# An SSD scan regrouped: 16 steps of two heads and both chunks, with the running sums broadcast by rounded 256-column products

## The chip, the cores and the metric

The kernel runs on one core of a Trainium2 chip. The metric is the device time of one execution in microseconds (us); the time before is the median of 3 runs. Engine names are those of the profile: PE (matrix products; PEld is its weight load), DVE (vector), ACT (scalar, activation functions), POOL (GpSimd), SP (queue of transfers).

## The reference, cut to what matters

The whole program is a transformer block with three mixers (DSA, NSA and SSD) and two further blocks, for 256 tokens of width 1024. The change is in the SSD mixer: 32 heads of 64 channels, 4 groups, state 128, and two chunks of 128 tokens.

```python
a_cum = jnp.cumsum(dtc * a, axis=2)                      # per head, within a chunk
seg = a_cum[:, :, :, None] - a_cum[:, :, None, :]
lmat = jnp.exp(jnp.where(tril, seg, -jnp.inf))           # 128 x 128 per head and chunk
cb = jnp.einsum('bcign,bcjgn->bcijg', cm, bm)            # per group
y_diag = jnp.einsum('bcijg,bcijgh,bcjgh,bcjghp->bcighp', cb, lmat, dtc, xs)
...
y_off = jnp.einsum('bcign,bcghpn,bcigh->bcighp', cm, h_in, jnp.exp(a_cum))
y = y_diag + y_off + xs * d_skip.reshape(SSD_GROUPS, SSD_HPG)[:, :, None]
y = rms_norm(y * jax.nn.silu(z.astype(jnp.float32)), norm_g)
```

`h_in` is zero for the first chunk, so `y_off` exists for the second chunk alone.

## The kernel before, in words

Activations stand transposed, channels on the partitions and the 256 tokens along the free axis, in `arena`. A dense layer is a row of jobs; a job makes 128 output channels out of 8 (`br_ssd`: 16) weight blocks. Each block takes three products of rounded operands (L1835 to L1837: rounded weight by rounded input, rounded weight by the input's remainder, the weight's remainder by rounded input), so a usual job is 24 products of 256 columns. Weights come in units of 8 blocks into a ring of five (`ring`). Two jobs ahead of its use ACT rounds a unit (`ring_hi`, L914), and POOL or DVE makes the remainder (`ring_lo`, L579): POOL for all units of `br_dsa`, POOL and DVE in turns for `mg` and `br_nsa`.

The order of all work is one list, `schedule()`; each engine walks through it and takes its own part of each entry, in order, with waits on semaphores. The stretch of interest has the jobs `mg` 20 to 23 (gates), `br_dsa` 0 to 7 and `br_nsa` 0 to 7 (projections of the two attention outputs), then `br_ssd`, which needs the finished SSD output. Between the jobs stands `filler`, groups of small work; its last 21 groups (`quads`) are the scan. The list puts one group behind each job, two at a few places: behind `mg` 23 stand groups 3 and 4, behind `br_dsa` 6 groups 11 and 12. Behind `mg` 23 stand also the roundings of the DSA output (`split dsa`, ACT L937), whose remainders (L587) are made by POOL for odd and by DVE for even chunks. The first job of `br_dsa` waits for each of them as it comes to the chunk; chunks 1 and 3 belong to a pair of POOL instructions before two scan steps in its queue, 5 and 7 to a pair behind them.

A scan step has four heads of one chunk; steps 0 to 7 are chunk 0, steps 8 to 15 chunk 1:
- uA (PE, L1741): for each head a product of a broadcast column of `dta` (the increments) and the upper triangle; it puts the running sum on all partitions, 128x128 in PSUM. These are full fp32 products; the profile shows two records for each.
- uE, one group later (ACT): four L899 (relu of the difference, 128 columns), for chunk 1 the exponential of the sums into `sbuf_t` (L904), then the exponential of all four (L907). POOL multiplies: `sbuf_t` by C (L710, chunk 1 alone) and `sbuf_s` by `cbt` (L714).
- uB, three groups after uA: PE multiplies by `xd` (L1755) and for chunk 1 by the state `hst` (L1758), into one bank (`p_pv`); DVE adds the skip term (L1435) and multiplies by the gate (L1440).
- Once chunk 1 of a head pair is done, the output is squared (ACT L967), rounded (ACT L935), its remainder made (DVE L1178), and the squares are summed on PE (ysum, L1767). Each of these exists 16 times.

uA has two banks (`p_score`), uB one, so uA of step i needs ACT's reads of step i-2, and uB of step i needs DVE's of step i-1.

Of the kernel before, what the change touches and what calls it, by code (L numbers as in the profile page):

```python
# [5 lines left out]
F32 = mybir.dt.float32  # L6
# [5 lines left out]
P = 128  # L12
S = 256
# [83 lines left out]
def schedule():  # L97
# [228 lines left out]
def psum_tenants(steps):  # L326
# [8 lines left out]
    for s in steps:  # L335
# [33 lines left out]
def program(nc, x_t, w_stream, w_tok, w_cmp, w_rgi, cols, rows, out):  # L369
# [24 lines left out]
    with ExitStack() as ctx:  # L394
# [60 lines left out]
        dec = sb("dec", [P, 32])  # L455
        half = sb("half", [P, 180])
# [146 lines left out]
        CONSTS, ZEROS, IKZ_ZEROS = 5 + 4 * 16, 21, 17  # L603
# [29 lines left out]
        def _(pool):  # L633
# [44 lines left out]
            for s in steps:  # L678
# [23 lines left out]
                elif k == "uE":  # L702
                    i = s[1]
                    t, hq = i // 8, i % 8
                    g = hq // 2
                    l = sbuf_s[:, i % 4, :].rearrange("p (h i) -> p h i", h=4)
# [7 lines left out]
                    pool.tensor_tensor(  # L714
                        l, l, cbt[:, t, P * g:P * g + P].unsqueeze(1).to_broadcast([P, 4, P]),
# [42 lines left out]
        def _(act):  # L758
# [27 lines left out]
            for s in steps:  # L786
# [1133 lines left out]
```

## Time and profile before

| | before |
|---|---|
| median of 3 runs | 1085.75 us (1085.55 to 1087.79) |
| the profiled execution | 1085.7 us, all of it span |
| PE busy | 1042.7 us, 96% |
| DVE, ACT, POOL busy | 695.8, 610.4, 588.5 us |
| mean granted clock of PE | 0.992 |
| the scan, first uA to the job behind the last ysum | 394.4 to 487.3 us |

Busy time counts an engine's instructions; matrix products overlap each other by about their latency, so what one costs in a row of many is the distance of starts, and a PE that shows as busy all the time isn't at its peak. The granted clock is the share of full speed that PE had.

### The profile page before, as it was taken

The numbers are of one execution on the slowest core, as the hardware profiler recorded it, in microseconds if no ns is written. First come the engines' busy times: TensorE is split into PE (matmuls) and PEld (weight loads), VectorE is DVE, ScalarE is ACT, GpSimd is POOL, SyncE is SP. The second block draws the span as 40 slices with busy tenths as digits, with TensorE's granted clock in tenths as the row PEclk, the third lists the DMA queues.
The fourth block names the chain that finished last, engine by engine and source line by source line (L and its number), as shares of the span: only waits on it lengthen the run. The fifth ranks groups of instructions, "written<-read, shape, count | busy, mean of one in ns | idle before, by whom it ended". The sixth has DMA issues, their size and how long they took to land.

```text
span 1085.7 us, 21365 instructions
## 1 busy us (share of the span) xinstructions
PE 1042.7 (96%) x8145; PEld 979.9 (90%) x8145; DVE 695.8 (64%) x1467; ACT 610.4 (56%) x1237; POOL 588.5 (54%) x448
## 2 busy tenths in 40 slices
PE   8999999999999999999999999999999998899896
PEld 8799988988889898989999999999899988889896
DVE  7869576666664425685485553332799976788864
ACT  5454557666665447764455655444434446568953
POOL 3656345454454459645534344346768875467652
PEclk9999899999999999999999999999999999999999
DMA  8234333333234442324555555555444543634442
GB/s 311 96 120 151 100 115 108 107 117 117 99 102 131 139 138 96 98 98 155 182 168 175 178 190 177 187 182 175 158 166 162 175 151 123 212 124 149 148 163 78
DMA packets 43157, 158.08 MB, mean 146 GB/s; under 512 B 4912, under 2 KB 4912, under 8 KB 42672
## 3 DMA queue, kind: packets, MB, share of 16 engines
q1 hardware_dynamic: 42912, 156.69, 43.5%
q8 instruction: 65, 1.06, 0.4%
q14 instruction: 36, 0.29, 0.1%
q10 hardware_dynamic: 144, 0.03, 0.0%
HBM read 155.65 MB, written 1.05 MB: 144 GB/s over the span
## 4 chain that ended last, share of the span: by engine, by line
PE 73%; DVE 14%; ACT 6%; issue 3%; POOL 2%; DMA 1%; DVEq 0%; ACTq 0%; SPq 0%; POOLq 0%
PE p_proj L1835 20%; PE p_proj L1836 19%; PE p_proj L1837 19%; PE p_score L1673 4%; PE p_proj L1820 3%; PE p_pv L1701 2%; DVE ring_lo L579 2%; ACT ring_hi L914 2%; DVE arena_r L1178 2%; PE p_turn L1683 1%; POOL ring_lo L579 1%; DVE arena L1399 1%; PE p_score L1593 1%; PE p_score L1741 1%; DVE arena_r L587 1%
## 5 line engine op out<-in xcount | busy, mean ns | idle before, releaser
L1835 PE MATMUL p_proj<-arena_r,ring_hi 128*128 128x256 f32 x2208 | 654.9, 297 | 18.8 <-POOL ring_lo L579 10.5
L1836 PE MATMUL p_proj<-arena_r,ring_hi 128*128 128x256 f32 x2208 | 626.7, 284 | 0.0
L1837 PE MATMUL p_proj<-arena_r,ring_lo 128*128 128x256 f32 x2208 | 626.3, 284 | 0.0
L579 POOL TENSOR_TENSOR ring_lo<-ring,ring_hi 128x1024 fp32r<-128x1024 f32 x178 | 427.9, 2407 | 291.7 <-ACT ring_hi L914 290.8
L1835 PEld LDWEIGHTS p_proj<-arena_r,ring_hi 128*128 128x128 f32 x2208 | 424.9, 192 | 38.1 <-issue 21.4
L1836 PEld LDWEIGHTS p_proj<-arena_r,ring_hi 128*128 128x128 f32 x2208 | 425.4, 193 | 7.4 <-issue 6.0
L1837 PEld LDWEIGHTS p_proj<-arena_r,ring_lo 128*128 128x128 f32 x2208 | 425.1, 193 | 0.0
L914 ACT ACTIVATE ring_hi<-ring 128x1024 fp32r<-128x1024 f32 x276 | 290.3, 1052 | 94.4 <-PE p_proj L1837 91.4
L579 DVE TENSOR_TENSOR ring_lo<-ring,ring_hi 128x1024 fp32r<-128x1024 f32 x98 | 125.1, 1276 | 71.9 <-ACT ring_hi L914 70.4
L688 POOL TENSOR_TENSOR sbuf_s<-sbuf_s,srow 128x256 f32<-128x256 f32 (+1 forms) x48 | 41.7, 870 | 83.1 <-DVE srow L1381 58.2
L937 ACT ACTIVATE arena_r<-arena 128x256 fp32r<-128x256 f32 x108 | 42.4, 409 | 39.8 <-DVE arena L1552 22.3
L587 POOL TENSOR_TENSOR arena_r<-arena,arena_r 128x256 fp32r<-128x256 f32 x59 | 46.3, 803 | 21.9 <-ACT arena_r L937 21.9
L935 ACT ACTIVATE arena_r<-arena,par 128x256 fp32r<-128x256 f32 x48 | 23.6, 504 | 56.8 <-DVE arena L1559 43.7
L1369 DVE CUSTOM_DVE_ANT_0 sbuf_s<-p_score,caus,nrq 128x128 f32<-128x128 f32 (+1 forms) x64 | 24.2, 415 | 40.9 <-PE p_score L1673 40.8
L1070 ACT ACTIVATE th<-p_proj 128x256 f32<-128x256 f32 x44 | 16.8, 382 | 57.9 <-PE p_proj L1837 57.9
L1559 DVE TENSOR_TENSOR arena<-arena,p_proj 128x256 f32<-128x256 f32 x40 | 16.9, 421 | 49.3 <-PE p_proj L1837 48.4
L1472 DVE SCALAR_TENSOR_TENSOR p_score<-arena,par,p_score 128x256 f32<-128x256 f32 x116 | 47.0, 483 | 1.2
L860 ACT ACTIVATE sbuf_s<-sbuf_s,srow 128x128 f32<-128x128 f32 (+1 forms) x96 | 42.6, 449 | 3.1 <-DVE srow L1369 3.1
L1178 DVE SCALAR_TENSOR_TENSOR arena_r<-arena,par,arena_r 128x256 fp32r<-128x256 f32 x48 | 36.8, 766 | 11.0 <-ACT arena_r L935 9.6
L587 DVE TENSOR_TENSOR arena_r<-arena,arena_r 128x256 fp32r<-128x256 f32 x49 | 29.2, 596 | 15.5 <-ACT arena_r L937 13.8
L1820 PE MATMUL p_proj<-arena,ring 128*128 128x256 f32 x160 | 36.5, 381 | 2.1 <-ACT p_proj L1058 1.1
L1192 DVE SCALAR_TENSOR_TENSOR arena<-p_proj,rinv 128x256 f32<-128x256 f32 x32 | 13.6, 425 | 37.5 <-PE p_proj L1837 37.4
(287 smaller groups left out, 1163.9 us busy)
## 6 DMA issues: line engine op xcount, KB each, us to landing
ring<-w_stream SPq DMA_DIRECT2D x286, 512.0 KB, 3.3
arena<-w_tok SPq DMA_DIRECT2D x1, 1632.0 KB, 12.8
arena<-w_rgi SPq DMA_DIRECT2D x1, 1536.0 KB, 6.4
arena<-x_t SPq DMA_DIRECT2D x4, 256.0 KB, 6.5
arena<-w_cmp SPq DMA_DIRECT2D x1, 1024.0 KB, 15.7
out_t<-arena SPq DMA_DIRECT2D x4, 256.0 KB, 2.6
par<-cols SPq DMA_DIRECT2D x1, 323.0 KB, 3.3
row<-rows ACTq DMA_DIRECT2D x1, 32.0 KB, 3.5
```

Source lines behind the costliest of these rows:

```text
L579: return eng.tensor_tensor(ring_lo[:, u % RING, :, :].rearrange("p k n -> p (k n)"), ring[:, u % RING, :, :].rearrange("p k n -> p (k n)") ...
L587: return eng.tensor_tensor(lo(c), src(c), hi(c).bitcast(F32), ALU.subtract)
L860: ins = act.activation(p, p, ACT.Exp, bias=srow[:, i % 4, 2 + h:3 + h], scale=-1.0, accum_out=srow[:, i % 4, 4 + h:5 + h])
L914: act.activation(ring_hi[:, hi_slot[u], :, :].rearrange("p k n -> p (k n)"), ring[:, u % RING, :, :].rearrange("p k n -> p (k n)"), ACT.Copy)\
L937: ins = act.activation(hi(c), src(c), ACT.Copy)
L1178: dve.scalar_tensor_tensor(out=lo(c), in0=src(c), scalar=col(GAIN[tag], c), in1=hi(c).bitcast(F32), op0=ALU.mult, op1=ALU.subtract)\
L1472: ins = dve.scalar_tensor_tensor(out=A(AC + cc) if tap == CONV_K - 1 else acc, in0=ub[:, cc, tap:tap + S], scalar=col("even_cw", CONV_K * ...
L1673: pe.matmul(ps, A(q + c)[:, P * t:P * t + P], kk[:, :, 0:kl], start=True, stop=True)\
L1820: mm = pe.matmul(slot(s)[:, 0:S], ring[:, u % RING, b % 8, :], rhs[c], start=(c == 0), stop=(c == n - 1))
L1835: pe.matmul(slot(s)[:, 0:S], w_hi, hi, start=(c == 0), stop=False)
L1836: pe.matmul(slot(s)[:, 0:S], w_hi, lo, start=False, stop=False)
L1837: mm = pe.matmul(slot(s)[:, 0:S], w_lo, hi, start=False, stop=(c == n - 1))
```

## The change

The 16 steps are cut the other way: two heads and both chunks in each. uA becomes two products of 256 columns: a column of `pick` (rounded, an identity in its upper 32 partitions and again in the next 32), broadcast, by `acum_t`. `acum_t` holds the transposed running sums of both chunks, the rounded part of the 32 heads on partitions 0 to 31 and the remainder on 32 to 63, so that one product adds both up. It is made once, where the running sums were made before (`acum`), by one more product on PE, two copies on ACT and two subtractions on DVE; ACT copies `pick` there, and two fills are added on DVE. In every step ACT takes an exponential of 256 columns into `sbuf_t` and POOL a product of 256 columns. uB has four products by `xd` and two by `hst`; DVE has two instructions of 256 columns in place of four of 128. The output of a head pair is now ready after each step, so `split y`, `ysq`, `ysum` and `lo y` come one at a time in every group from the fourth on, not two at a time in the last eight.

```diff
-        if 8 <= i - 4 < 16:
-            for c in (2 * (i - 12), 2 * (i - 12) + 1):
-                group += [("ysum", c), ("lo", "y", c)]
-        if 8 <= i - 3 < 16:
-            for c in (2 * (i - 11), 2 * (i - 11) + 1):
-                group += [("split", "y", c), ("ysq", c)]
+        if 0 <= i - 4 < 16:
+            group += [("ysum", i - 4), ("lo", "y", i - 4)]
+        if 0 <= i - 3 < 16:
+            group += [("split", "y", i - 3), ("ysq", i - 3)]
...
                     pool.wait_ge(sem("l_ready"), i + 1)
-                    if t == 1:
-                        e = sbuf_t[:, i % 2, :].rearrange("p (h i) -> p h i", h=4)
-                        link(pool.tensor_tensor(e, e, A(XB + 20 + g)[:, P:S].unsqueeze(1).to_broadcast([P, 4, P]),
-                                                ALU.mult))
+                    link(pool.tensor_tensor(e, e, A(XB + 20 + g)[:, P:S].unsqueeze(1).to_broadcast([P, 2, P]),
+                                            ALU.mult))
...
                     ps = take(s)
+                    for t in range(NT):
+                        act.activation(acum_t[0:32, P * t:P * t + P], ps[32 * t:32 * t + 32, P:S], ACT.Copy)
...
+                    for r in (0, 32):
+                        ins = act.activation(pick[r:r + 32, :], ident[r:r + 32, r:r + 32], ACT.Copy)
...
-                    if t == 1:
-                        if i >= 10:
-                            act.wait_ge(sem("pv_done"), 48 + i - 1)
-                        ins = act.activation(sbuf_t[:, i % 2, :], ps, ACT.Exp)
-                    ins.then_inc(read["score", "A"], 1); note(read["score", "A"])
+                    if i >= 2:
+                        act.wait_ge(sem("pv_done"), 48 + i - 1)
+                    act.activation(sbuf_t[:, i % 2, 0:S].rearrange("p (h i) -> p h i", h=2),
+                                   ps.rearrange("p (h t i) -> p h t i", h=2, t=NT)[:, :, 1, :], ACT.Exp)\
+                        .then_inc(read["score", "A"], 1); note(read["score", "A"])
...
+                    for t in range(NT):
+                        ins = dve.tensor_tensor(acum_t[32:64, P * t:P * t + P], ps[32 * t:32 * t + 32, P:S],
+                                                acum_t[0:32, P * t:P * t + P].bitcast(F32), ALU.subtract)
...
+                    pe.matmul(ps[0:64, P:S], dta[:, :], upper[:, :], start=True, stop=True)
...
-                    for h in range(4):
-                        n = 32 * t + 4 * hq + h
-                        mm = pe.matmul(slot(s)[:, P * h:P * h + P], dta[:, n:n + 1].to_broadcast([P, P]),
-                                       upper[:, :], start=True, stop=True)
...
+                    for h in range(2):
+                        n = 2 * i + h
+                        mm = pe.matmul(slot(s)[:, S * h:S * h + S], pick[:, n:n + 1].to_broadcast([P, P]), acum_t[:, :],
+                                       start=True, stop=True)
```

How the instructions now stand is shown at two places. The first is PE between job `mg` 23 and the first product of `br_dsa` 0: before, steps 3 and 4 of uA with steps 0 and 1 of uB (`p_score` is uA's output, `p_pv` uB's).

```order
L1741 MATMUL p_score<-upper,dta 128x128 x4
L1755 MATMUL p_pv<-sbuf_s,arena 64x128 x4
L1741 MATMUL p_score<-upper,dta 128x128 x4
L1755 MATMUL p_pv<-sbuf_s,arena 64x128 x4
L1835 MATMUL p_proj<-arena_r_51,ring_hi 128x256
```
and now:
```order
L1747 MATMUL p_score<-acum_t,pick 128x256 x2
L1763 MATMUL p_pv<-sbuf_s,arena 64x128 x4
L1767 MATMUL p_pv<-sbuf_t,arena 64x128 x2
L1747 MATMUL p_score<-acum_t,pick 128x256 x2
L1763 MATMUL p_pv<-sbuf_s,arena 64x128 x4
L1767 MATMUL p_pv<-sbuf_t,arena 64x128 x2
L1776 MATMUL p_mean<-th,mean_d 128x256
L1844 MATMUL p_proj<-arena_r_51,ring_hi 128x256
```
Each uA is two wide products; the products by `hst` are there from the first step on, and a ysum (L1776, `p_mean`) stands ahead of the job.

The second is POOL, from the product of step 0 to the second pair of DSA remainders. L579 is a weight remainder, L722 a gate of `mg`, L587 the pairs of DSA remainders, L714 the product by `cbt`; before:

```order
L714 TENSOR_TENSOR sbuf_s<-sbuf_s,kk_s 128x512
L579 TENSOR_TENSOR ring_lo<-ring,ring_hi 128x1024
L722 TENSOR_SCALAR sqb<-sqb 128x256
L714 TENSOR_TENSOR sbuf_s<-sbuf_s,kk_s 128x512
L579 TENSOR_TENSOR ring_lo<-ring,ring_hi 128x1024
L722 TENSOR_SCALAR root<-root 128x256
L587 TENSOR_TENSOR arena_r_55<-arena,arena_r_51 128x256 x2
L714 TENSOR_TENSOR sbuf_s<-sbuf_s,kk_s 128x512 x2
L587 TENSOR_TENSOR arena_r_56<-arena,arena_r_52 128x256 x2
```
and now (the same lines are L581, L723, L589 and L715; L711 is the product of `sbuf_t` by C):
```order
L711 TENSOR_TENSOR sbuf_t<-sbuf_t,arena 128x256
L715 TENSOR_TENSOR sbuf_s<-sbuf_s,kk_s 128x512
L581 TENSOR_TENSOR ring_lo<-ring,ring_hi 128x1024
L723 TENSOR_SCALAR sqb<-sqb 128x256
L711 TENSOR_TENSOR sbuf_t<-sbuf_t,arena 128x256
L715 TENSOR_TENSOR sbuf_s<-sbuf_s,kk_s 128x512
L581 TENSOR_TENSOR ring_lo<-ring,ring_hi 128x1024
L723 TENSOR_SCALAR root<-root 128x256
L589 TENSOR_TENSOR arena_r_55<-arena,arena_r_51 128x256 x2
L711 TENSOR_TENSOR sbuf_t<-sbuf_t,arena 128x256
L715 TENSOR_TENSOR sbuf_s<-sbuf_s,kk_s 128x512
L711 TENSOR_TENSOR sbuf_t<-sbuf_t,arena 128x256
L715 TENSOR_TENSOR sbuf_s<-sbuf_s,kk_s 128x512
L589 TENSOR_TENSOR arena_r_56<-arena,arena_r_52 128x256 x2
```
Ahead of the pair that makes chunks 5 and 7 stand four instructions more, one for each of steps 0 to 3.

## Rows read from the trace of the kernel before

**Rows 1.** The page: busy time by engine, granted clock in 40 slices, chain by engine
```profile
PE 1042.7 (96%) x8145; PEld 979.9 (90%) x8145; DVE 695.8 (64%) x1467; ACT 610.4 (56%) x1237; POOL 588.5 (54%) x448
...
PEclk9999899999999999999999999999999999999999
...
PE 73%; DVE 14%; ACT 6%; issue 3%; POOL 2%; DMA 1%; DVEq 0%; ACTq 0%; SPq 0%; POOLq 0%
```

**Rows 2.** Windows of two stretches: us, busy us by engine, granted clock, DMA share, GB/s
```profile
411.00:416.00 5.00, 4.40 (x34) 3.79 (x33) 3.50 (x8) 4.97 (x13) 5.00 (x5) 1.00 0.01 3
...
488.00:492.00 4.00, 4.00 (x25) 4.00 (x24) 2.58 (x3) 2.53 (x3) 2.55 (x1) 0.64 0.00 0
```

**Rows 3.** Timeline of PE: rows of the stretch with idle time before them
```profile
408.81 1.16 PE L1741 MATMUL p_score<-upper,dta 128*128 128x128 f32 x8 [1.44 <-ACT sbuf_s L899]
...
413.08 0.39 PE L1835 MATMUL p_proj<-arena_r,ring_hi 128*128 128x256 f32 x1 [0.60 <-DVE arena_r L587]
...
445.09 1.16 PE L1741 MATMUL p_score<-upper,dta 128*128 128x128 f32 x8 [0.69 <-ACT sbuf_t L904]
...
486.21 1.41 PE L1767 MATMUL p_mean<-th,mean_d 128*128 128x256 f32 x4 [1.65 <-ACT th L967]
```

**Rows 4.** Timeline of PE: start, length; br_dsa jobs 1 to 3, step of first chunk
```profile
416.57 0.38 PE L1835 MATMUL p_proj<-arena_r,ring_hi 128*128 128x256 f32 x1
...
421.11 0.39 PE L1835 MATMUL p_proj<-arena_r,ring_hi 128*128 128x256 f32 x1
...
424.09 1.05 PE L1741 MATMUL p_score<-upper,dta 128*128 128x128 f32 x8
...
425.07 0.66 PE L1755 MATMUL p_pv<-sbuf_s,arena 128*64 128x128 f32 x8
...
425.66 0.39 PE L1835 MATMUL p_proj<-arena_r,ring_hi 128*128 128x256 f32 x1
```

**Rows 5.** Timeline of PE: starts of jobs and products where chunk 1 is computed
```profile
439.30 0.39 PE L1835 MATMUL p_proj<-arena_r,ring_hi 128*128 128x256 f32 x1
...
448.03 0.47 PE L1835 MATMUL p_proj<-arena_r,ring_hi 128*128 128x256 f32 x1
...
452.07 0.45 PE L1755 MATMUL p_pv<-sbuf_s,arena 128*64 128x128 f32 x4
...
453.14 1.13 PE L1767 MATMUL p_mean<-th,mean_d 128*128 128x256 f32 x4
...
453.92 0.47 PE L1835 MATMUL p_proj<-arena_r,ring_hi 128*128 128x256 f32 x1
...
465.71 0.47 PE L1835 MATMUL p_proj<-arena_r,ring_hi 128*128 128x256 f32 x1
...
487.27 0.56 PE L1835 MATMUL p_proj<-arena_r,ring_hi 128*128 128x256 f32 x1
```

**Rows 6.** Timeline of POOL from its first product of a step
```profile
400.56 1.30 POOL L714 TENSOR_TENSOR sbuf_s<-sbuf_s,kk_s 128x512 f32<-128x512 f32 x1 [1.29 <-ACT sbuf_s L907]
...
408.67 1.57 POOL L587 TENSOR_TENSOR arena_r<-arena,arena_r 128x256 fp32r<-128x256 f32 x2
...
410.21 2.53 POOL L714 TENSOR_TENSOR sbuf_s<-sbuf_s,kk_s 128x512 f32<-128x512 f32 x2
...
412.70 1.79 POOL L587 TENSOR_TENSOR arena_r<-arena,arena_r 128x256 fp32r<-128x256 f32 x2
...
414.45 2.37 POOL L579 TENSOR_TENSOR ring_lo<-ring,ring_hi 128x1024 fp32r<-128x1024 f32 x1
```

**Rows 7.** Groups of instructions by line and shape, POOL and ACT
```profile
L688 POOL TENSOR_TENSOR sbuf_s<-sbuf_s,srow 128x256 f32<-128x256 f32 x24 | 15.7, 656 | 37.6 <-DVE srow L1381 27.0 <-DVE srow L1377 10.6
...
L710 POOL TENSOR_TENSOR sbuf_t<-sbuf_t,arena 128x512 f32<-128x512 f32 x8 | 10.8, 1348 | 11.7 <-ACT sbuf_s L907 11.4
...
L869 ACT ACTIVATE sbuf_t<-p_turn 128x256 f32<-128x256 f32 x24 | 9.0, 376 | 0.3 <-PE p_turn L1683 0.2
```

**Rows 8.** Timeline of ACT: the exponential that waits for uB
```profile
444.44 0.60 ACT L904 ACTIVATE sbuf_t<-p_score 128x512 f32<-128x512 f32 x1 [4.06 <-PE p_pv L1758]
```

More of the change, by code:

```diff
@@ L357, in psum_tenants @@
             add("pv", s, "D")
-        elif k in ("norm", "acum", "ynorm"):
+        elif k in ("norm", "ynorm"):
             add("mean", s, "A")
+        elif k == "acum":
+            add("mean", s, "AD")
         elif k == "qsq":
@@ L714, in _ @@
                     pool.tensor_tensor(
[L715 removed]
+                        l, l, cbt[:, :, P * g:P * g + P].unsqueeze(1).to_broadcast([P, 2, NT, P]),
                         ALU.mult).then_inc(sem("m_ready"), 1); note(sem("m_ready"))
@@ L1247, in _ @@
                     was_read(dve, s)
+                    ps = slot(s)
+                    for t in range(NT):
+                        ins = dve.tensor_tensor(acum_t[32:64, P * t:P * t + P], ps[32 * t:32 * t + 32, P:S],
+                                                acum_t[0:32, P * t:P * t + P].bitcast(F32), ALU.subtract)
+                    ins.then_inc(read["mean", "D"], 1); note(read["mean", "D"])
                     dve.tensor_tensor(dec[:, :], ac[:, 64:96], ac[:, 0:32], ALU.subtract)\
@@ L1426, in _ @@
                     i = s[1]
-                    t, hq = i // 8, i % 8
                     dve.wait_ge(sem("pv_done"), 48 + i + 1)
-                    ps = slot(s)
+                    ps = slot(s)[:, 0:S]
                     if i == 0:
                         dve.wait_ge(read["proj", "D"], gate_reads[15])
-                    for cc in range(2):
-                        c = 2 * hq + cc
-                        xs = A(XB + c)[:, P * t:P * t + P]
-                        ins = dve.scalar_tensor_tensor(out=ps[:, P * cc:P * cc + P], in0=xs, scalar=col("ssd_d", c),
-                                                       in1=ps[:, P * cc:P * cc + P], op0=ALU.mult, op1=ALU.add)
-                    link(ins)
-                    for cc in range(2):
-                        c = 2 * hq + cc
-                        ins = dve.tensor_tensor(A(XB + c)[:, P * t:P * t + P], ps[:, P * cc:P * cc + P],
-                                                A(SZ + c)[:, P * t:P * t + P], ALU.mult)
-                    ins.then_inc(read["pv", "D"], 1); note(read["pv", "D"])
+                    link(dve.scalar_tensor_tensor(out=ps, in0=A(XB + i), scalar=col("ssd_d", i), in1=ps,
+                                                  op0=ALU.mult, op1=ALU.add))
+                    dve.tensor_tensor(A(XB + i), ps, A(SZ + i), ALU.mult)\
+                        .then_inc(read["pv", "D"], 1); note(read["pv", "D"])
                 elif k == "ynorm":
@@ L1751, in _ @@
                         was_read(pe, ("xtr", 7), "D")
-                    for h in range(4):
-                        head = 4 * hq + h
-                        o = slot(s)[64 * (h % 2):64 * (h % 2) + 64, P * (h // 2):P * (h // 2) + P]
-                        mm = pe.matmul(o, xd[t][:, 64 * head:64 * head + 64], sbuf_s[:, i % 4, P * h:P * h + P],
-                                       start=True, stop=(t == 0), skip_group_check=True)
-                        if t == 1:
-                            mm = pe.matmul(o, hst[:, 64 * head:64 * head + 64], sbuf_t[:, i % 2, P * h:P * h + P],
-                                           start=False, stop=True, skip_group_check=True)
+                    l = sbuf_s[:, i % 4, :].rearrange("p (h t i) -> p h t i", h=2, t=NT)
+                    o = [[slot(s)[64 * h:64 * h + 64, P * t:P * t + P] for t in range(NT)] for h in range(2)]
+                    for t in range(NT):
+                        for h in range(2):
+                            head = 2 * i + h
+                            pe.matmul(o[h][t], xd[t][:, 64 * head:64 * head + 64], l[:, h, t, :],
+                                      start=True, stop=(t == 0), skip_group_check=True)
+                    for h in range(2):
+                        head = 2 * i + h
+                        mm = pe.matmul(o[h][1], hst[:, 64 * head:64 * head + 64], sbuf_t[:, i % 2, P * h:P * h + P],
+                                       start=False, stop=True, skip_group_check=True)
                     mm.then_inc(sem("pv_done"), 1)
```

33 lines of the change are left out of this document (18 added, 15 removed).

## The prediction

> **What bounds the kernel now.** The page first: PE is busy 96% of the span and carries 73% of the chain that ended last, mostly the job products; its clock is near full speed throughout [rows 1]. So time is won on PE, or in the waits that PE has. The timeline of PE over the scan has both. In the even part a job and its step follow each other without a gap: jobs start at 416.57, 421.11 and 425.66, 4.54 us apart, of which 2.98 is the 24 products, 0.98 uA and 0.59 uB [rows 4]. From chunk 1 on, a step costs more: 1.07 us of uB and 0.78 of two ysum products, against 0.98 for uA as before [rows 5]. The waits stand at the two places with two groups behind one job (408.81 and 413.08; 445.09) and at the last ysum, 486.21 [rows 3]. Behind the last one the clock is down: 0.64 of full speed over 488 to 492, that is 1.2 GHz for most of it, which costs about 4 x 0.36 = 1.4 us. Behind the first two it stayed at 1.00 [rows 2]. The fourth thing to see is POOL: in 411 to 416 it is busy 5.00 of 5.00 us [rows 2], and its rows from 400.56 to 414.45 follow each other without a named wait, up to the pair of DSA remainders that ends at 12.70 + 1.79 = 414.49 [rows 6] (the rest of `br_dsa` 0, which ends some 2 us before 416.57, needs them).
>
> **uA.** Gone are 0.98 us a step. In its place come two rounded 256-column products; the nearest rows are the job products, 2.98/24 = 0.124 us each, plus the 0.09 that uA shows beyond its eight records at 0.111 (the change to the 64-row products of uB) [rows 4]: 0.34. A saving of 0.64 a step, 10.2 us over 16. Bounds: no saving below the two products' 0.25 (11.7 us in all); if a broadcast rounded column streamed at the fp32 product's pace, two of 256 columns would cost what four of 128 do and nothing is won. The weight operand is broadcast before as well and shows no cost, so I take 0.64.
>
> **uB and ysum on PE.** Before 8 steps at 0.59 and 8 at 1.07, 13.3 us; now 16 with six products for eight or four, the mean 0.83, 13.3 again. The two halves of the heads still alternate. Ysum: 8 x 0.78 becomes 16 singles; half of 0.78 plus a change of operand shape is 0.42 to 0.45 [rows 5], so +0.5 to +1.0 us.
>
> **ACT.** Each step has an exponential of 256 columns, 0.38 us by the nearest row [rows 7], for 0.60 in eight steps [rows 8]: +1.3 us in total. It lies beside PE, but it comes before the bank of uA is free, and from step 2 on it waits for a uB as the one at 444.44 does [rows 8].
>
> **POOL.** Here the change costs. The product of `sbuf_t` exists now for steps 0 to 7 too. A 256-column POOL product took 0.66 (one small operand), a 512-column one 1.35 [rows 7], and a 1024-column one 2.37 [rows 6]: I take 0.72 and 0.08 for its link, 0.80. Four of them stand ahead of the second pair of DSA remainders: +3.2 us. POOL starts its first step 0.25 us earlier (uA 0.64 shorter, 0.4 of exponential more ahead of it). The pair ends at 414.49 + 3.2 - 0.25 = 417.4. PE, which comes to the job at about 409.5, stands idle in it for some 5 us with a few products between. Bounds: 0.66 gives 417.0, 1.35 gives 419.9. The Trainium skill, "GPSIMD Engine Reference", section on elementwise cycle accounting, has 4497 ns for 2048 fp32 columns of a two-input operation, which would make this one 0.56 us before its fixed part; by it the pair ends near 417.0, and the rows of this case decide it.
>
> **The walk**, as the shift of job starts against before. `br_dsa` 1: behind 417.4 come three products, uA 0.34, uB 0.83, ysum 0.45, so 419.4 for 416.57: **+2.8**. The next five jobs are 2.98 + 0.34 + 0.83 + 0.45 = 4.60 apart for 4.54: +3.1 at `br_dsa` 6. To the next job before 8.73 us (439.30 to 448.03 [rows 5]). Now the job and step 2.98 + 0.34 + 0.83, then uA has to wait for the exponential that waits for uB, about 0.5; uB 0.83 starts 1.1 behind the last one, and its ysum waits for ACT until 2.45 behind it: 2.98 + 0.34 + 0.83 + 2.45 = 6.6 in all. **+1.0.** Then three intervals, from 448.03 to 465.71, 5.89 each, become 4.60: **-2.9**. From 465.71 to 487.27 [rows 5], 21.56 us before with the waits at 479 and 486.21; now three intervals without uA, 2.98 + 0.83 + 0.45 + 0.15 of drain = 4.4, and one of 3.5: 16.7. **-7.8.** The wait at 486.21 goes because DVE and ACT have one head pair a group to finish there, not two. The low clock behind it goes too: -1.4, **-9.2**. But a wait as long as that in `br_dsa` 0 should bring the low clock to what follows it, +1.4 (0 to 2.8, since the wait at 486.21 did so and those at 408.81 and 413.08 didn't): **-7.8**. The Trainium skill, "TensorE: Matmul & The Clock Gate", section on how waits throttle, says the same: an engine that waits between bursts restarts at the low clock. At the start, one more product, +0.3 on PE at the running sums; its ACT and DVE copies and the fills lie under the first `mg` jobs, if not +1: with 0.2 for the fills **-7.3**.
>
> Behind 487 nothing changes, PE is the chain [rows 1], and the shift reaches the end. The profiled execution took 1085.7, as the median of 1085.75: **1078.4 us**.
>
> **Rivals.**
> - *POOL is not late.* If DVE and ACT, not POOL, end the wait in `br_dsa` 0 (POOL's product cheaper, or its chain had slack in waits that no row names), the job ends near 414 and not 417.7: 3.5 us less and no new low clock, 1.4 less: 1073.3. For it: in the trace before, the named wait there is DVE's (413.08). Against: POOL's rows leave no room. 0.17.
> - *The waits spread.* The low clock holds for two stretches, or DVE, which shares its stretch with a POOL that is never idle now, is slower: +3 to +4: 1082. 0.18.
> - *Slower than before: POOL sets the pace of all `br_dsa` jobs.* A step costs it 2.37 for the ring remainder and up to 1.49 for the `cbt` product, as now, plus x and 0.16. PE's pace is 4.60. With x = 0.72 POOL needs 4.7 at worst and has some 4 us in hand (remainders are made two jobs ahead). Each us of x costs 4 us at the first job and 8 over the next eight; to eat 7.3 us of gain and the 4 in hand x has to reach 1.7, above the 1.35 of twice the columns. 1088. 0.05.
> - *The product is no faster*, the other bound of uA: the 10.2 us stay, and POOL's cost remains: 1088. 0.02. *Part of it*: the gain is eaten to within 0.2%: 0.05.
>
> **How the numbers follow.** Forecast 0.53, the others as given. A measurement of this kernel tells about 0.2%, 2.2 us. Faster are the first three cases, 0.88; within 0.2% one, 0.05; slower the two at 1088, 0.07. The range goes from the first rival to the second, 1072.8 to 1082.3; it leaves out the rest, somewhat under 2 in 10.
>
> **What would show it.** L1747 in 32 products about 0.12 apart; PE idle in `br_dsa` 0 with POOL's L589 as the releaser, the job's last product near 417.5; L711 at 0.7; no wait of over 1 us at the last ysum; jobs 4.6 apart from `br_dsa` 1 to `br_nsa` 1; a stretch of low clock moved from 488 to about 417. The forecast fails if L589 is done by 415, or if new waits for ACT's exponential stand in each step (its loop from uB through exponentials, rounding, square, ring and relus is near PE's pace).

## The result and the profile after

| | median us | range, runs | ratio to before |
|---|---|---|---|
| before | 1086.22 | 1084.01 to 1089.09, 20 | |
| changed | 1088.38 | 1086.35 to 1090.79, 20 | 1.0019, interval 1.0012 to 1.0027 |

The change makes the kernel 2.2 us slower (0.2%, and the interval lies above 1), where 1078.4 was forecast. Both profiles are of executions above the median: a span is 1.7 to 1.8 us shorter than the time of its run throughout, so the 1085.7 us of before is the span of a run of about 1087.5, and the 1087.4 of after is that of a run of 1089.12. The page of after, as [rows 1]: busy time, granted clock by slices, chain.

```profile
PE 1038.1 (95%) x8051; PEld 973.8 (90%) x8051; DVE 702.1 (65%) x1439; ACT 612.4 (56%) x1249; POOL 592.8 (55%) x456
...
PEclk9999899999999998899999999999999999999999
...
PE 71%; DVE 15%; ACT 5%; POOL 4%; issue 3%; DMA 1%; DVEq 0%; ACTq 0%; SPq 0%; POOLq 0%
```

PE has 4.6 us less to do and still ends later: its share of the chain fell from 73 to 71%, POOL's rose from 2 to 4%. The clock row has two 8s about 40% into the span, in the scan, where before had 9s. What PE waits for in 396 to 500 us (us in total, times, longest):

```profile
PE p_score L1747 <- ACT sbuf_t L909: 4.2, 2, 2.3
PE p_pv L1763 <- DVE arena L1444: 3.5, 5, 0.9
PE p_proj L1844 <- POOL arena_r L589: 3.4, 1, 3.4
PE p_mean L1776 <- ACT th L973: 0.3, 1, 0.3
```

The wait at the last ysum is down from 1.65 us [rows 3] to 0.3, as forecast; the others add up to 11.1. Two long ones stand at `br_dsa` 0 (the timeline of PE has 2.32 at 408.48, in the scan groups just ahead of the job, and 3.42 at 418.01, inside it), 1.85 and four of under 1 us at 440 to 457. The windows of three stretches with low clock (us, busy us by engine, clock, DMA share, GB/s):

```profile
410.00:414.00 4.00, 4.00 (x25) 3.40 (x21) 2.37 (x4) 3.97 (x14) 3.92 (x6) 0.57 0.02 4
417.00:424.00 7.00, 5.99 (x30) 5.26 (x31) 2.25 (x5) 1.71 (x4) 4.59 (x5) 0.52 0.22 75
454.50:461.30 6.80, 5.50 (x27) 4.70 (x28) 4.73 (x9) 5.74 (x16) 3.78 (x4) 0.50 0.00 0
```

Each is most of the time at 1.2 GHz and stands at or behind one of the waits. The starts of jobs on PE's timeline, as [rows 4, 5]: `br_dsa` 1, 4, 5, 6, 7 and `br_nsa` 6, with the waits of the stretch in which the time goes:

```profile
422.79 0.78 PE L1844 MATMUL p_proj<-arena_r,ring_hi 128*128 128x256 f32 x1
...
436.84 0.47 PE L1844 MATMUL p_proj<-arena_r,ring_hi 128*128 128x256 f32 x1
...
439.89 0.39 PE L1747 MATMUL p_score<-acum_t,pick 128*128 128x256 f32 x2
...
441.67 0.47 PE L1844 MATMUL p_proj<-arena_r,ring_hi 128*128 128x256 f32 x1
...
447.22 0.47 PE L1844 MATMUL p_proj<-arena_r,ring_hi 128*128 128x256 f32 x1
...
451.57 0.66 PE L1763 MATMUL p_pv<-sbuf_s,arena 128*64 128x128 f32 x8 [0.90 <-DVE arena L1444]
...
452.42 0.70 PE L1776 MATMUL p_mean<-th,mean_d 128*128 128x256 f32 x2
...
454.97 0.80 PE L1747 MATMUL p_score<-acum_t,pick 128*128 128x256 f32 x2 [1.85 <-ACT sbuf_t L909]
...
456.59 1.12 PE L1763 MATMUL p_pv<-sbuf_s,arena 128*64 128x128 f32 x8 [0.83 <-DVE arena L1444]
...
458.73 0.77 PE L1844 MATMUL p_proj<-arena_r,ring_hi 128*128 128x256 f32 x1
...
490.45 0.47 PE L1844 MATMUL p_proj<-arena_r,ring_hi 128*128 128x256 f32 x1
```

From `br_dsa` 5 at 441.67 to 6 at 447.22 it is 5.55 us, and from 447.22 to 458.73 it is 11.51, where before took 8.73 [rows 5]. A uA is two records there, 0.39 us with their drain.

The first uA stands at 395.63 in this profile and at 394.44 in that of before. In the fourteen kernels profiled here it lies anywhere from 393.1 to 395.6, old steps and new, so this 1.2 us can't be put down to the change. From here on, places are counted from each kernel's first uA ("from uA"). `br_nsa` 6 starts 92.8 from uA before and 94.8 after. From there to the end of the span before took 598.4 us and after takes 597.0.

### The profile page after: what moved, and what is told of

It is laid out like the page before. It is cut to its first block, busy times and chain, and to the rows that moved or that the text cites. A ratio compares the mean times of both kernels' runs of the same rounds, so it can differ in the third digit from the quotient of the medians.

```text
span 1087.4 us, 21170 instructions
## 1 busy us (share of the span) xinstructions
PE 1038.1 (95%) x8051; PEld 973.8 (90%) x8051; DVE 702.1 (65%) x1439; ACT 612.4 (56%) x1249; POOL 592.8 (55%) x456
## 4 chain that ended last, share of the span: by engine, by line
PE 71%; DVE 15%; ACT 5%; POOL 4%; issue 3%; DMA 1%; DVEq 0%; ACTq 0%; SPq 0%; POOLq 0%
PE p_proj L1844 19%; PE p_proj L1845 18%; PE p_proj L1846 18%; PE p_score L1677 4%; PE p_proj L1829 3%; ACT ring_hi L920 2%; DVE arena_r L1184 2%; PE p_pv L1705 2%; DVE ring_lo L581 2%; POOL ring_lo L581 2%; PE p_turn L1687 1%; DVE arena L1410 1%; PE p_score L1596 1%; DVE arena_r L589 1%; POOL arena_r L589 1%
## 5 line engine op out<-in xcount | busy, mean ns | idle before, releaser
L581 POOL TENSOR_TENSOR ring_lo<-ring,ring_hi 128x1024 fp32r<-128x1024 f32 x178 | 429.8, 2417 | 285.0 <-ACT ring_hi L920 284.0
L920 ACT ACTIVATE ring_hi<-ring 128x1024 fp32r<-128x1024 f32 x276 | 290.1, 1052 | 87.2 <-PE p_proj L1846 83.7
L581 DVE TENSOR_TENSOR ring_lo<-ring,ring_hi 128x1024 fp32r<-128x1024 f32 x98 | 124.2, 1267 | 72.0 <-ACT ring_hi L920 70.6
L943 ACT ACTIVATE arena_r<-arena 128x256 fp32r<-128x256 f32 x108 | 42.4, 408 | 40.1 <-DVE arena L1555 22.7
L941 ACT ACTIVATE arena_r<-arena,par 128x256 fp32r<-128x256 f32 x48 | 23.8, 507 | 61.0 <-DVE arena L1562 42.8
L589 POOL TENSOR_TENSOR arena_r<-arena,arena_r 128x256 fp32r<-128x256 f32 x59 | 45.9, 793 | 22.2 <-ACT arena_r L943 22.2
L1184 DVE SCALAR_TENSOR_TENSOR arena_r<-arena,par,arena_r 128x256 fp32r<-128x256 f32 x48 | 45.8, 953 | 10.6 <-ACT arena_r L941 8.9
L589 DVE TENSOR_TENSOR arena_r<-arena,arena_r 128x256 fp32r<-128x256 f32 x49 | 32.8, 670 | 15.5 <-ACT arena_r L943 14.0
```

The lines of the kernel that those rows point to most:

```text
L581: return eng.tensor_tensor(ring_lo[:, u % RING, :, :].rearrange("p k n -> p (k n)"), ring[:, u % RING, :, :].rearrange("p k n -> p (k n)") ...
L589: return eng.tensor_tensor(lo(c), src(c), hi(c).bitcast(F32), ALU.subtract)
L920: act.activation(ring_hi[:, hi_slot[u], :, :].rearrange("p k n -> p (k n)"), ring[:, u % RING, :, :].rearrange("p k n -> p (k n)"), ACT.Copy)\
L943: ins = act.activation(hi(c), src(c), ACT.Copy)
L1184: dve.scalar_tensor_tensor(out=lo(c), in0=src(c), scalar=col(GAIN[tag], c), in1=hi(c).bitcast(F32), op0=ALU.mult, op1=ALU.subtract)\
```

## Where the time goes: a ring through DVE and ACT

DVE in the stretch of the 5.5 us jobs, of after (start, length; L589 is the remainder of a `split nsa`, L1442 and L1444 are uB's part, L1184 is `lo y`):

```profile
437.08 2.35 DVE L589 TENSOR_TENSOR arena_r<-arena,arena_r 128x256 fp32r<-128x256 f32 x1 [0.48 <-ACT arena_r L943]
439.47 0.49 DVE L1442 SCALAR_TENSOR_TENSOR p_pv<-arena,par,p_pv 128x256 f32<-128x256 f32 x1
439.99 0.42 DVE L1444 TENSOR_TENSOR arena<-p_pv,arena 128x256 f32<-128x256 f32 x1
...
442.62 2.36 DVE L589 TENSOR_TENSOR arena_r<-arena,arena_r 128x256 fp32r<-128x256 f32 x1 [0.49 <-ACT arena_r L943]
```

ACT there (L941 `split y`, L973 `ysq`, L920 the rounding of a weight unit, L943 `split nsa`):

```profile
440.45 0.51 ACT L941 ACTIVATE arena_r<-arena,par 128x256 fp32r<-128x256 f32 x1 [1.51 <-DVE arena L1444]
440.87 0.40 ACT L973 ACTIVATE th<-arena 128x256 f32<-128x256 f32 x1
441.17 1.04 ACT L920 ACTIVATE ring_hi<-ring 128x1024 fp32r<-128x1024 f32 x1
442.12 0.40 ACT L943 ACTIVATE arena_r<-arena 128x256 fp32r<-128x256 f32 x1
```

and POOL:

```profile
436.75 2.40 POOL L581 TENSOR_TENSOR ring_lo<-ring,ring_hi 128x1024 fp32r<-128x1024 f32 x1 [0.89 <-ACT ring_hi L920]
...
442.29 2.41 POOL L581 TENSOR_TENSOR ring_lo<-ring,ring_hi 128x1024 fp32r<-128x1024 f32 x1 [0.90 <-ACT ring_hi L920]
```

Follow it round: DVE L589 until 439.43, L1442 and L1444 until 440.41; ACT waits for that, then 0.42 + 0.30 + 0.95 + 0.40 by starts until 442.52; L589 again at 442.62. That is 5.54 us from 437.08, and PE, with 4.5 of work, waits in it. The ring is as long as it is because of L589: 2.35 us for an instruction that takes 0.43 at 455.13, where POOL does nothing. Each time it ends just behind POOL's L581 (439.43 behind 439.15; 444.98 behind 444.70). The trace names no wait of one for the other. The Trainium skill, "SBUF — State Buffer", section "Who interferes with whom", states that a DVE instruction with two SBUF inputs contends with a GpSimd instruction that reads SBUF, that this contention is an exclusive lock, and that the order of issue decides which of the two is blocked. The trace agrees: L589 starts 0.33 us behind L581 and ends 0.28 behind its end, where 0.43 would be expected, as far as ends of POOL can be trusted. ring_split below has L589 with and without an L581 beside it. And ACT releases L581 and L589 right behind each other (442.29 and 442.62), so the collision repeats itself in each round. In this ring DVE is busy 4.90 of the 5.54 us, ACT 4.00 and POOL 4.56. In before the steps of these jobs have no `split y`, `ysq` or `lo y`, so ACT's `split nsa` waits for no uB, and there is no ring.

## The experiments

All are compared with before, which ran again beside them: its median was 1086.35 us beside y_late, nsa_behind, dsa_first and both_moved, 1086.5 beside no_e, ring_split, spread and before_spread, 1086.48 beside the others. For the changed kernel the median is that of the table, 1088.38. "At `br_dsa` 0" takes in the scan groups ahead of that job; "gap" is idle time ahead of an instruction on PE's timeline.

**y_late.** The changed kernel with the y work back in the last eight groups, two at a time:

```diff
-        if 0 <= i - 4 < 16:
-            group += [("ysum", i - 4), ("lo", "y", i - 4)]
-        if 0 <= i - 3 < 16:
-            group += [("split", "y", i - 3), ("ysq", i - 3)]
+        if 8 <= i - 4 < 16:
+            for c in (2 * (i - 12), 2 * (i - 12) + 1):
+                group += [("ysum", c), ("lo", "y", c)]
+        if 8 <= i - 3 < 16:
+            for c in (2 * (i - 11), 2 * (i - 11) + 1):
+                group += [("split", "y", c), ("ysq", c)]
```

> The changed kernel with one part undone: rounding, square, sum and remainder of the SSD output stand again two at a time in the last eight groups, not one in every group from the fourth on. Theory L (a loop): the 5.54 us between jobs from br_dsa 4 to 6 is a closed loop DVE remainder of the NSA output (2.36, held while POOL works) -> DVE uB (0.98) -> ACT rounding and square of y (0.8) -> ACT ring_hi (1.04) -> ACT rounding of the NSA output (0.4) -> DVE again. Without y in it ACT is free 0.8 us earlier, so jobs br_dsa 1 to 6 stand about 4.5 us apart with no wait of uB for DVE; the wait in br_dsa 0 shortens by at most 1 us. In the br_nsa part the two-at-a-time waits come back (some 4 to 5 us). Rival P (POOL's e product alone): the jobs stay 5.5 apart, since POOL has the same work. L: 1084 to 1088; P: 1090 to 1093.

Measured: 1086.0 us, 1084.7 to 1086.96 (10 runs), ratio 0.9992 (0.9979 to 1.0004). The ring is gone: `br_dsa` 1 to 6 stand 4.1 us apart, the double group takes 10.0 us instead of 11.5 and `br_nsa` 6 starts 90.4 from uA. The double group still has a gap, of 1.86 us, now for POOL's product by `cbt`. The long waits at `br_dsa` 0 stay (gaps of 2.30 and 2.76 us), with 10.2 us of low clock around the second. The waits of 4 to 5 us expected in the `br_nsa` part didn't come back: `br_nsa` 2 to 6 takes 17.9 us for 17.0. The scan is 4.4 us shorter, the time 2.4: behind it stands a new gap of 1.96 us (see tail_swap).

**nsa_behind.** `split nsa` behind the scan group, not ahead of it, so that it stands behind ACT's `split y` with the weight unit behind both:

```diff
         for n, job in enumerate(wide):
...
-        if job[1] == "br_dsa":
-            out.append(("split", "nsa", job[2]))
         want = (n + 1) * len(filler) // (len(wide) - 2)
...
+        if job[1] == "br_dsa":
+            out.append(("split", "nsa", job[2]))
```

> The changed kernel with the rounding and remainder of an NSA chunk moved behind the scan group of its job, so that DVE does uB first. Theory L: uB no longer stands behind a remainder that POOL holds up; jobs br_dsa 3 to 6 come 4.6 us apart, the wait of 1.85 us at the double group behind br_dsa 6 shrinks to under 1, and the low clock there goes: 5 to 8 us less than the changed kernel, 1081 to 1083. Rival P: DVE is held in uB's place too or ACT is the pace, jobs stay at 5.5: 1088. The wait in br_dsa 0 is untouched by both (18.6 us after the first uA + 4.5).

Measured: 1083.76 us, 1082.79 to 1084.77 (6 runs), ratio 0.997 (0.9956 to 0.9984). All the work is there, in another order, and `br_dsa` 2 to 6 stand 4.53 us apart; the double group takes 7.8. `br_nsa` 6: 88.5 from uA. DVE and POOL there:

```profile
441.75 0.69 DVE L589 TENSOR_TENSOR arena_r<-arena,arena_r 128x256 fp32r<-128x256 f32 x1 [0.19 <-ACT arena_r L943]
```

```profile
438.89 2.38 POOL L581 TENSOR_TENSOR ring_lo<-ring,ring_hi 128x1024 fp32r<-128x1024 f32 x1
...
443.55 2.37 POOL L581 TENSOR_TENSOR ring_lo<-ring,ring_hi 128x1024 fp32r<-128x1024 f32 x1
```

L589 no longer meets L581 (it lies between the two, partly beside an L711), and takes 0.69 us. The time is just above the expected 1081 to 1083. This is the test of the ring: one entry of the list moved by one group takes 6.3 us out of the scan and 4.6 off the time.

**ring_split.** The weight remainders of `br_dsa` in turns on POOL and DVE (`"br_dsa"` taken out of the list of names that POOL does alone):

> The changed kernel with the weight remainders of br_dsa made by POOL and DVE in turns, as for mg and br_nsa, not by POOL alone. POOL has 4 x 2.4 us less. Theory L: in jobs where POOL has no ring_lo the NSA remainder of DVE takes 0.42 and not 2.36, and POOL comes to the DSA remainders 2.4 us earlier: the mean distance of jobs br_dsa 3 to 6 falls under 5.0, br_dsa 1 starts 2 us earlier. DVE has 1.24 more in every second job, which may take that back. 1082 to 1085. Rival (the pace is ACT's, through its wait of the exponential for uB): 5.5 stays, 1088.

Measured: 1085.37 us, 1082.59 to 1088.2 (10 runs), ratio 0.9993 (0.9977 to 1.0008). Distances of `br_dsa` 1 to 6: 4.5 three times, 4.9, 5.0; the double group 11.2. `br_dsa` 1 starts 3.3 us earlier, since POOL is relieved. DVE, with no POOL instruction beside the first and an L581 on POOL from 431.41 beside the second:

```profile
428.13 0.42 DVE L589 TENSOR_TENSOR arena_r<-arena,arena_r 128x256 fp32r<-128x256 f32 x1
...
431.74 2.35 DVE L589 TENSOR_TENSOR arena_r<-arena,arena_r 128x256 fp32r<-128x256 f32 x1 [0.24 <-ACT arena_r L943]
```

The next three are 0.43, 2.36 and 0.43, again by whether POOL has an L581: the same instruction, in the same place of the list, is long only beside POOL's. From one L589 to the next it is then 3.6 us behind a short one and 7.0 behind a long one (with a remainder of 1.23 us on DVE in it). Half the collisions are left, and half of what the single jobs lost; the double group keeps its loss. The time can't be told from before's.

**no_e.** POOL's product of `sbuf_t` (L711) is left out in all steps, so the state's part lacks its factor C:

```diff
-                    link(pool.tensor_tensor(e, e, A(XB + 20 + g)[:, P:S].unsqueeze(1).to_broadcast([P, 2, P]),
-                                            ALU.mult))
```

> The changed kernel without POOL's product of the exponentials by C (L711) in all 16 steps; this leaves that factor of the state's contribution out of the output, so its time is a bound and not a version. Theory P (POOL's added products are the loss): POOL's second pair of DSA remainders ends 3.5 to 4 us earlier (4 x 0.9), the wait in br_dsa 0 shrinks by that, the low clock behind it too, and the jobs from br_dsa 4 on return to 4.6 us: 1080. Theory L (the DVE remainder is held by POOL's 2.4 us ring_lo, not by the product): br_dsa 0 gains the same 3.5 us, but the jobs run back into the 5.5 us loop: 1084 to 1086.

Measured: 1087.52 us, 1086.54 to 1089.43 (10 runs), ratio 1.0011 (1.0001 to 1.0021). `br_dsa` 1 starts 23.1 from uA instead of 27.2: what POOL's product does at `br_dsa` 0 is 4.1 us, the term forecast at 2.9 and its low clock at 1.4. But the ring doesn't care: 5.5 us jobs from `br_dsa` 4 on, double group 11.5. `br_nsa` 6 starts 90.2 from uA, 4.6 us earlier than in the changed kernel, and the time is 0.9 less: 1.77 go in the gap behind the scan, and more stretches of low clock stand later on (behind `br_nsa` 6 some 18 us in this profile, against 6 in that of after). The jobs came as the second theory had them, the time didn't (1084 to 1086). Taking away the cost that I had priced left the kernel no faster than before.

**dsa_first.** All eight `split dsa` ahead of scan groups 3 and 4 (four stood behind them):

```diff
-            out += [("split", "dsa", c) for c in range(4)]
+            out += [("split", "dsa", c) for c in range(8)]
...
-        if job == mg[23]:
-            out += [("split", "dsa", c) for c in range(4, 8)]
```

> The changed kernel with all eight roundings and remainders of the DSA output ahead of the two scan groups behind mg 23, not four ahead and four behind. POOL makes chunks 5 and 7 before its four products of steps 2 and 3, 4.6 us earlier. If the wait in br_dsa 0 is POOL's queue (as predicted), it falls from 3.4 us to under 1, br_dsa 1 starts 5 us earlier and the low clock over 417 to 424 goes: 1081 to 1083. If DVE and ACT were about to end it as well: 1086. The loop at br_dsa 4 to 6 stays, and could eat part of it, since it has a pace of its own (5.54 for each of more jobs): then 1084 to 1085.

Measured: 1088.57 us, 1087.25 to 1089.8 (10 runs), ratio 1.0017 (1.0005 to 1.003). `br_dsa` 1 at 24.6 from uA, 2.6 earlier; the ring eats most of it (`br_nsa` 6 at 94.1, after 94.8), and the time is none of the three expected. The wait on POOL is gone, and longer waits for ACT and DVE stand in the same place (3.52 and 2.42 us), so POOL's queue was late, but the other two were close behind it.

**both_moved.** dsa_first and nsa_behind together.

> Both moves at once. If the POOL wait and the loop are two separate causes the gains add: 1074 to 1078, the time that was first predicted or less. If one hides the other (what is won at the first is lost at the loop), nearer 1081.

Measured: 1081.7 us, 1080.77 to 1083.07 (4 runs), ratio 0.9948 (0.9929 to 0.9967). `br_nsa` 6 at 86.2. With the ring open the earlier start counts: 2.1 us in the time, where dsa_first alone was worth nothing. That is the second of the two cases expected, nearer 1081.

**spread** and **before_spread.** nsa_behind, and no two scan groups behind one job: one group for each job from `mg` 20 on. The first on the changed kernel, the second on the kernel before.

```diff
+        want = min(want, len(soft) + len(prep) + max(0, n + 1 - wide.index(mg[20])))
         while at < min(want, len(filler)):
```

> The changed kernel with the NSA rounding behind the scan group, and one scan group behind each job from mg 20 on, so no job has two. No work is changed. PE then has a job of 3 us between any two steps: the waits of 3.5 and 2.2 us (or 2.3 and 0.6) between steps 3 and 4, and those behind br_dsa 6, go, and POOL's pair for chunks 5 and 7 stands behind one step less (2.2 us). The wait inside br_dsa 0 is then POOL's alone, 1 to 2 us. First uA to the job behind the last ysum: 80 us, against 88.5 with the NSA move alone: 1075 to 1078. If the chain of one step (uB to DVE to ACT to POOL) is longer than a job, new waits of about 1 us per job keep it at 1082.

> The kernel before, with the same two moves (NSA rounding behind the group, one group behind each job). It says what of the gain of the run before this one belongs to the order and what to the new steps. Before has no closed loop in br_dsa, so the NSA move brings nothing; the spread takes away its waits of 1.4, 0.8 and 0.7 us, 3 in all. In the br_nsa part the two-at-a-time work stands one job later. 1082 to 1085. The new steps are then worth what the two runs differ by: if PE's saving of 0.64 us a step shows once the waits are gone, 6 to 9 us.

Measured: spread 1082.96 us, 1079.06 to 1083.82 (9 runs), ratio 0.9957 (0.9945 to 0.997); before_spread 1089.95 us, 1085.99 to 1091.16 (10 runs), ratio 1.0022 (1.0007 to 1.0037). In the same order the new steps are 7.0 us faster than the old. Both expected ranges were missed: spread is hardly better than nsa_behind alone (1083.76, ranges overlap), and the order makes the old steps slower. Without the double groups the waits at `br_dsa` 0 become, in spread, 4.2 and 0.7 us for POOL's remainders: `br_dsa` 0 now comes earlier than they can be there.

**ua_alone.** The kernel before with `acum_t`, `pick` and their making, and uA alone changed, to products of 128 columns:

```diff
                     for h in range(4):
-                        n = 32 * t + 4 * hq + h
-                        mm = pe.matmul(slot(s)[:, P * h:P * h + P], dta[:, n:n + 1].to_broadcast([P, P]),
-                                       upper[:, :], start=True, stop=True)
+                        n = 4 * hq + h
+                        mm = pe.matmul(slot(s)[:, P * h:P * h + P], pick[:, n:n + 1].to_broadcast([P, P]),
+                                       acum_t[:, P * t:P * t + P], start=True, stop=True)
```

> The kernel before, whose sixteen steps stay as they were (four heads, one chunk, y work two at a time at the end), with one part of the change: the transposed running sums in acum_t, the pick matrix, and uA as four rounded products of 128 columns instead of four fp32 ones. It asks what the product alone is worth and whether the closed loop of DVE and ACT needs the new steps. Theory A (the saving of the product is real and passes to the end where PE is the bound; the loop of 5.5 us comes only of the y work in every step): uA from 0.98 to 0.3-0.5 us a step, jobs 4.0-4.2 us apart where they stood 4.54 apart, last ysum 5 to 8 us earlier, 1079-1083 us at the end since 1.5 us or so are given back to the wait for DVE's weight remainder behind the scan. Theory B (the old steps had their own chain, and PE's saving turns into waits for ACT and DVE at once): uA shorter, but jobs still about 4.5 us apart with gaps ahead of uA or the jobs, 1084.5-1087 us. If a product of 128 columns is no faster than fp32 (0.9 us a step), both fall and the saving belongs to the 256 columns: 1086 us.

Measured: 1084.06 us, 1082.3 to 1089.27 (11 runs), before beside it 1086.48 (1084.24 to 1088.32, 23 runs), ratio 0.9982 (0.9969 to 0.9994). PE's timeline:

```profile
430.26 0.56 PE L1760 MATMUL p_score<-acum_t,pick 128*128 128x128 f32 x4
430.74 0.66 PE L1774 MATMUL p_pv<-sbuf_s,arena 128*64 128x128 f32 x8
431.33 0.38 PE L1854 MATMUL p_proj<-arena_r,ring_hi 128*128 128x256 f32 x1
...
434.30 0.56 PE L1760 MATMUL p_score<-acum_t,pick 128*128 128x128 f32 x4
```

uA is 0.48 us by starts (four products at 0.12), jobs 4.04 apart, with no ring. So the rounded product wins 0.5 us a step at once in the old steps. 4.9 us of it are left at `br_nsa` 6 (87.9 from uA), and 2.4 at the end: new gaps stand ahead of a later uB (1.90 at 469.6, for DVE) and behind the scan (1.96 at 489.8). The expected range of 1079 to 1083 was missed: the second eight steps don't pass the gain on.

**early_dve.** both_moved, and two of POOL's weight remainders (units 88 and 89, used by `br_dsa`) on DVE, which is idle from 393 to 404 there:

```diff
         def on_gpsimd(u):
+            if u in (88, 89):
+                return False
```

> The changed kernel with both earlier moves (split nsa behind the filler group, all eight dsa splits ahead of groups 3 and 4: 1081.7 us) and two weight remainders, those of the units that POOL works at 401.7 and 406.5 us, on DVE, which is idle from 393.2 to 404.5 us there. Theory A (POOL, 0.8 us longer in each step by the state product, is full from 401 us on, and its two remainders of 2.4 us hold the dsa remainders, the masks of uB and with them the first br_dsa jobs; DVE has room): the gaps of 3.5 and 2.2 us at 408 and 411 us become under 2 in sum, br_dsa 1 stands at 21-23 us from the first uA (25.4 now), the low clock of 10.2 us behind them shortens to 3.4-6.8, nsa6 at 82-84 (86.2), 1077.5-1079.5 us. Theory B (what starts the jobs is ACT's eight splits and DVE's own queue, POOL only the last named): gaps stay within 1 us of now, 1081-1082.5 us.

Measured: 1080.14 us, 1079.64 to 1081.06 (5 runs), ratio 0.9946 (0.9933 to 0.9958). `br_nsa` 6 at 84.7, `br_dsa` 1 at 23.9 (25.4): the second gap at `br_dsa` 0 went from 2.16 to 1.20, the first, for ACT's exponential, stayed at 3.5. Less than expected. DVE and POOL hold each other up here as well; DVE's L581 of 2.23 us against 1.23 for the next:

```profile
400.64 2.23 DVE L581 TENSOR_TENSOR ring_lo<-ring,ring_hi 128x1024 fp32r<-128x1024 f32 x1 [7.36 <-ACT ring_hi L920]
...
403.83 1.23 DVE L581 TENSOR_TENSOR ring_lo<-ring,ring_hi 128x1024 fp32r<-128x1024 f32 x1 [0.97 <-ACT ring_hi L920]
```

**tail_swap** and **before_all.** Behind the scan, PE waits 1.7 us in both_moved for the weight remainder of `br_ssd` 0's first unit. DVE there:

```profile
480.94 2.52 DVE L1182 SCALAR_TENSOR_TENSOR arena_r<-arena,par,arena_r 128x256 fp32r<-128x256 f32 x1
483.49 1.76 DVE L1446 RECIPROCAL p_mean<-root 128x256 f32<-128x256 f32 x1
485.28 2.69 DVE L579 TENSOR_TENSOR ring_lo<-ring,ring_hi 128x1024 fp32r<-128x1024 f32 x1
```

tail_swap is early_dve with the two units changed over between the engines; before_all is the kernel before with every move of tail_swap.

```diff
+            if u in (104, 105):
+                return u == 104
```

> early_dve, and the remainders of the two weight units of br_ssd 0 changed over: the first on POOL, the second on DVE. In both_moved the PE waits 1.7 us at 488.1 for the first, which DVE does at 485.3 behind the y remainder that POOL holds at 2.5 us and the reciprocal that waits for ACT's root; POOL stood idle at 483.2. Theory A (this wait is where part of every gain in the scan is given back): it is gone or under 0.3 us, nothing takes its place, and the time is 1.3-1.8 us under that of early_dve, unless a stretch of low clock goes into its place. Theory B (the wait is of the norm chain as a whole, next late is the second unit or the gate product): a gap of over 1 us within 4 us behind, time within 0.5 us of early_dve.

> The kernel before, steps and fp32 products as they were, with all the moves of tail_swap (split nsa behind the filler group, eight dsa splits together, the two early remainders on DVE, the swap behind the scan). It says what of tail_swap's gain is the moves' and what the new steps'. Theory A (the new steps save the PE 10 us less some 1 of ysum, and only the order hid it): this kernel is 5 to 8 us slower than tail_swap, 1084-1087 us, uA 0.98 us a step, no gap of 5.5 us rhythm. Theory B (the moves do all of it, new steps no better than old): within 1.5 us of tail_swap.

Measured: tail_swap 1078.74 us, 1077.53 to 1080.53 (5 runs), ratio 0.9932 (0.992 to 0.9944); before_all 1086.22 us, 1084.14 to 1090.72 (12 runs), ratio 1.0001 (0.999 to 1.0012). What PE waits for in tail_swap, 396 to 500 us:

```profile
PE p_score L1749 <- ACT sbuf_t L911: 3.5, 1, 3.5
PE p_pv L1765 <- DVE arena L1446: 2.5, 2, 1.5
```

6.0 us of waits against 11.4 in the changed kernel, and none behind the scan. The remainder on DVE now takes 1.22 us there, for 2.69. tail_swap is the fastest version of this study, 7.7 us under before and 1.4 under early_dve. All its moves without the new steps are worth nothing (before_all); the new steps without the moves cost 2 us; together they gain.

## Why the prediction was wrong

**Right: uA.** It is 0.23 to 0.33 us a step by starts at full clock, forecast 0.34 (0.55 at 1.2 GHz, at 420.10). With one order for both, new steps beat old ones by 7.0 us (spread) and 7.5 (tail_swap); forecast for PE's own work was 10.2 less up to 1.0 for ysum, and the page shows 4.6 us less busy time, which counts products at 1.2 GHz at their longer time.

**Right: POOL in front of `br_dsa` 0.** L711 takes 0.72 to 1.01 us (taken at 0.80), and the second pair of remainders is where it was forecast:

```profile
412.52 0.92 POOL L711 TENSOR_TENSOR sbuf_t<-sbuf_t,arena 128x256 f32<-128x256 f32 x1
...
417.23 1.41 POOL L589 TENSOR_TENSOR arena_r<-arena,arena_r 128x256 fp32r<-128x256 f32 x2
```

It ends at 418.64; forecast was 417.4, with a first uA 1.2 us earlier. PE waits for it, as named. But it wasn't late alone: with it out of the way (dsa_first) `br_dsa` 1 comes only 2.6 us earlier.

**Right: the last third.** From `br_nsa` 2 to 6 the walk had 16.7 us for 21.6; it took 17.0, the wait at the last ysum went, and the low clock behind it too (1.00 over 488 to 492, for 0.64 in [rows 2]).

**Wrong.** The walk as shift of job starts against before, from uA:

| | forecast | measured |
|---|---|---|
| `br_dsa` 1 | +2.8 | +5.0 |
| `br_dsa` 6 | +3.1 | +6.7 |
| `br_dsa` 7 | +1.0 | +9.5 |
| `br_nsa` 2 | -2.9 | +6.6 |
| `br_nsa` 6 | -7.8 | +2.0 |

- The step that failed is "To the next job ... 6.6 in all", the double group behind `br_dsa` 6: 11.5 us. Of the 9.8 us missed at `br_nsa` 6 it has 4.9; 2.2 come up to `br_dsa` 1, 1.4 in the next five jobs, 1.0 up to `br_nsa` 2 (the first job takes 5.7 us, partly at 1.2 GHz) and 0.3 behind. The term that was too small is the 2.45 us from the end of the first uB to the next job, for which no row was given: it measured 6.3 (452.42 to 458.73). The other 1.0 is the gap ahead of the first uB. I summed PE's own work with one exponential and one ysum's wait. In fact both steps go round the ring through DVE and ACT, and PE waits in each: 0.90, 1.85 and 0.83 us, and from 454.5 on at 1.2 GHz. nsa_behind, which only opens the ring, brings it to 7.8.
- "The next five jobs are ... 4.60 apart" holds for two (4.5 us); the one before them takes 5.0, since it starts at 1.2 GHz, and from `br_dsa` 4 on they take 4.8 and 5.5. The last sentence of the prediction named a loop near PE's pace, of uB and ACT's queue, and waits for ACT's exponential in each step. It left out L589, and in the single steps PE waits for DVE (L1444), not for ACT.
- The low clock was forecast once, +1.4 in all. It came in three stretches, after the 2.32 us wait, after the 3.42 and after the 1.85; at `br_dsa` 1 alone it makes up most of the 2.2 us between forecast and measurement (from POOL's end to the job 4.15 us for 2.0). The second rival ("the waits spread") had both, a low clock for two stretches and a DVE that is slower beside POOL, at 3 to 4 us; the kernel came out 10.0 above the forecast.
- Of a gain in the scan, some 1.7 us are given back behind it (DVE's weight remainder) once the scan ends early; the profile of before couldn't show that wait, which its own low clock may have covered (no run tests that). It isn't there in the changed kernel, but in most of the versions with a shorter scan.
- Two small slips change nothing: with its link a POOL product of 0.66 gives 417.2, not 417.0, and the first rival comes to 1073.5, not 1073.3.

Not settled: how much of the ring's cost is L589's length and how much its place, since nsa_behind changes both at once; why the first gap at `br_dsa` 0, for ACT's exponential, stays at 3.5 us in early_dve and tail_swap, and how the later stretches of low clock (from 910 us on) come about, which differ from kernel to kernel with the same work there. The gain in the scan and the gain in the time differ by 1 to 2 us for most kernels, and by 3.7 for no_e; the gap behind the scan and these stretches are what the traces show for it.

## What to carry to other kernels

When work moves into every step of a loop over engines, add up the ring that it closes (each engine's queue from the result of one step to that of the next) and not only each engine's sum; here DVE was busy 65% and ACT 56% of the span, and even in the ring itself 88% and 72%, and their ring still set the pace. Price each instruction in that ring at its length beside whatever else runs at that time, since here a DVE instruction of 0.43 us, with two SBUF inputs, lasted as long as POOL's of 2.40. A change that shortens the bounding engine's work may need its neighbours in the list moved before it pays: neither the moves nor the new steps gained alone (the rounded product in the old steps gained 0.2%), and both together gave 0.7%.

## What the hardware showed that was not expected

- DVE's remainder of 256 columns: 0.43 us alone, 0.56 to 1.53 us in part beside a POOL instruction, 2.35 us when it starts 0.3 us behind POOL's weight remainder. The same for `lo y`: 0.48 alone and up to 2.52 us beside POOL. uB's first instruction, which reads PSUM and one SBUF operand, stayed at 0.49 throughout, beside POOL or not.
- A rounded product whose weight operand is one column broadcast runs at 0.12 us for 256 columns, and also 0.12 for 128 columns (ua_alone): what the chip gains there is the rounding, and the 256 columns halve the rest.
- Stretches at 1.2 GHz of 3.4 to 10.2 us stand at or behind every wait of 2.3 us and more that PE has in the scans of the fourteen kernels. Of the shorter waits some have one (1.65 at 486.21 in before, 1.77 at 492.12 in no_e, 1.85 in the changed kernel) and some don't (1.65 at 450.84 in before_spread, 1.96 at 492.34 in y_late): the length of one wait doesn't tell.
